# Streaming encoder step on one core: modulation by row blocks of w_ada on four column groups, with the low-rank projection in the same stage

## The reference

```python
mod = jax.nn.silu(c.astype(jnp.float32)) @ P['w_ada'][l] + P['b_ada'][l]
shift, scale, gate = jnp.split(mod[:, None, :], 3, axis=-1)
h = rms_norm(x, P['norm_g'][l]) * (1.0 + scale) + shift
proj = h @ P['w_in'][l]
pr, zA, cq, ckv, kr, zB, sq, sk, sv, zC, gates = _split(proj, IN_SIZES)
yA, S1, shift1 = rwkv7_branch(pr, shift0, S0, P, l)
...
xs = p_shift + (prev - p_shift) * P['rwkv_mu'][l]
r, k, v, wd, ad = _split(xs, RWKV_SIZES)
w_log = -jax.nn.softplus(-(P['rwkv_w0'][l] + jnp.tanh(wd) @ P['rwkv_w_up'][l])) - 0.5
```

## Time and profile before

| | |
|---|---|
| median of 3 runs | 4972.09 us (4970.42 to 4978.52) |
| the profiled execution | 4968.3 us, its span 4966.6 us |
| PE (TensorE, matmuls) busy | 4478.2 us, 90% |
| DVE (VectorE) busy | 2228.7 us, 45% |
| ACT (ScalarE) busy | 1621.3 us, 33% |
| POOL (GpSimd) busy | 722.7 us, 15% |
| mean granted TensorE clock | 0.959 of full speed |
| DMA, mean over the span | 59 GB/s |

### The profile page before, as it was taken

The page is one execution under the profiler, slowest core; times in us unless marked ns, Lnnn a source line. Parts: engine busy times, 40 slices in busy tenths (PEclk is TensorE's granted clock), DMA queues, the critical chain, the costliest instruction groups (busy, mean ns, idle before and its releaser), DMA issues. The chain is left out here.

```text
span 4966.6 us, 75992 instructions
## 1 busy us (share of the span) xinstructions
PE 4478.2 (90%) x29584; PEld 3069.2 (62%) x29584; DVE 2228.7 (45%) x4666; ACT 1621.3 (33%) x3854; POOL 722.7 (15%) x938
## 2 busy tenths in 40 slices
PE   6898888888989989999968898988899899899999
PEld 2556656556756667777425566565567666677774
DVE  2364555245544463434223556552455344634342
ACT  2332333345543341212023333333355333412110
POOL 0010010000001005543000100100000010055430
PEclk9998999999999999999989999999899999999999
DMA  5100110210012203232240101102100121132222
GB/s 213 26 13 22 33 14 23 81 48 25 16 49 74 63 23 127 87 104 73 82 171 26 14 25 29 16 21 81 51 22 15 49 85 56 33 118 98 99 78 68
DMA packets 151028, 291.40 MB, mean 59 GB/s; under 512 B 53332, under 2 KB 79188, under 8 KB 145830
## 3 DMA queue, kind: packets, MB, share of 16 engines
q1 hardware_dynamic: 150552, 281.75, 17.9%
q10 hardware_dynamic: 112, 4.72, 0.3%
HBM read 239.08 MB, written 52.06 MB: 59 GB/s over the span
## 5 line engine op out<-in xcount | busy, mean ns | idle before, releaser
L1014 PE MATMUL banks<-hT,w_piece 128*128 128x384 f32 x1536 | 560.7, 508 | 3.3 <-ACT raw L1118 3.1
L1014 PEld LDWEIGHTS banks<-hT,w_piece 128*128 128x128 f32 x1536 | 287.0, 198 | 178.5 <-issue 24.5
L2197 PE MATMUL banks<-hT,w_piece 128*128 128x384 f32 x1056 | 354.1, 489 | 1.4 <-ACT sb_gate_raw L2307 1.4
L2197 PEld LDWEIGHTS banks<-hT,w_piece 128*128 128x128 f32 x1056 | 196.1, 190 | 141.4 <-issue 16.6
L2548 PE MATMUL banks<-hT,mergedT 128*128 128x512 f32 x576 | 247.5, 592 | 0.0
L1963 DVE SCALAR_TENSOR_TENSOR keysT<-banks,gains,rstd 64x128 f32<-64x128 f32 (+1 forms) x272 | 112.1, 412 | 249.8 <-ACT rstd L1877 247.3
L2594 DVE TENSOR_TENSOR gate_quarters<-gate_kept,banks 128x288 f32<-128x288 f32 x144 | 65.4, 454 | 314.7 <-PE banks L2489 309.7
L2557 ACT ACTIVATE gate_kept<-banks 128x288 f32<-128x288 f32 x144 | 59.2, 411 | 437.0 <-PE banks L2489 437.0
L2548 PEld LDWEIGHTS banks<-hT,mergedT 128*128 128x128 f32 x576 | 109.4, 190 | 137.0 <-issue 136.8
L2369 DVE TENSOR_TENSOR_SCAN left<-pass,zero 128x384 f32<-128x384 f32 (+7 forms) x144 | 189.8, 1318 | 5.0
L2594 DVE TENSOR_TENSOR branch_quarters<-branch_kept,banks 128x288 f32<-128x288 f32 x144 | 65.5, 455 | 267.7 <-PE banks L2489 267.7
(11 more groups left out here) (386 smaller groups left out, 9552.3 us busy)
## 6 DMA issues: line engine op xcount, KB each, us to landing
w_piece<-in_w_cols SPq DMA_DIRECT2D x66, 512.0 KB, 4.6
w_ada<-in_w_ada SPq DMA_DIRECT2D x12, 2048.0 KB, 9.8
w_gate_ahead<-in_w_cols SPq DMA_DIRECT2D x48, 512.0 KB, 4.3
w_branch<-in_w_br SPq DMA_DIRECT2D x96, 256.0 KB, 2.8
w_gate<-in_w_cols SPq DMA_DIRECT2D x48, 512.0 KB, 4.3
y_branch<-y_gated SPq DMA_DIRECT2D x12, 1152.0 KB
sb_cached_keysT<-in_sbkT SPq DMA_DIRECT2D x8, 1024.0 KB, 7.1
sb_cached_values<-in_sbv SPq DMA_DIRECT2D x8, 1024.0 KB, 5.2
```

The source lines that it names most:

```text
L1014: last = mm(dst, w[0 if kind in ("k", "v") else 1][:, k, :], hT[:, k, c], start=(k == 0), stop=(k == KD - 1))
L2197: last = mm(ps[:, bank[n], 0:TG], w_of[wn][:, k, :], hT[:, k, TG * g:TG * g + TG], start=(k == 0), stop=(k == KD - 1))
```

## The change

- `c` is loaded, put through SiLU and turned in the stage of the constants, once for both layers, into `conditioningT`, whose 32 columns hold the nine and zeros. The load of `c` stands ahead of that of the constants.
- `w_ada` stays in rows. SyncE loads blocks of 128 rows by 2048 columns (shift and scale; 1 MB, four buffers), four ahead of x and four behind it. For each block TensorE does four matmuls, one for each 512 columns; the q-th writes PSUM partitions 32q to 32q + 31 of the same bank, so that the four use different groups of 32 columns of the array. Eight blocks accumulate. One addition of a 128 by 512 bias replaces four, and four transposes of 128 by 128 replace 16 small ones.
- The tiles of x are transposed behind the blocks k = 3 to 7, by the table `MOD_TILES`.
- The gate's 1024 columns come in four transfers of two row blocks each, as the buffers get free; group q holds the sum over rows 256q to 256q + 255. The bias is added to the four partial sums (it is zero except in group 0), and the matrices `selp` and `sels` add the groups while they spread the rows.
- The projection of the first `rwkv` stage moves into this stage, in three pieces between that work (`lora`); its tile order follows the scaling of `hT`. ScalarE evicts it and the gate rows. The stage of its own goes.
- The loads of `load_first` move into this stage, behind the gate's weights. The raw last columns are copied to `lora_ends` and stored from the next stage. The zeroing of `scores_r_sample` moves to GpSimd there.

```diff
-        with S.stage("consts_loaded",) as (block, sb, (consts_loaded,)):
+        cT = sbt("conditioningT", [P, KD, 32])
...
+                sp.dma_start(c[:, :], A["c_all"]).then_inc(c_loaded, 16)
                 sp.dma_start(cst[:, :], A["consts"][:, 0:CONST_RESIDENT]).then_inc(consts_loaded, 16)
...
+MOD_TILES = {3: (0, 1, 2), 4: (3, 4), 5: (5, 6), 6: (7,), 7: (8,)}
...
+            def load_w(k):
+                if k >= 4:
+                    sp.wait_ge(mod_used, k - 3)
+                sp.dma_start(w[k % 4][:, :], A["w_ada"][l, k, :, 0:2 * D]).then_inc(w_loaded[k % 4], 16)
...
+            for k in range(4):
+                load_w(k)
             sp.wait_ge(x_copied, 32)
...
+            for k in range(4, KD):
+                load_w(k)
+            sp.dma_start(w_lora[:, :, :], A["w_cols"][l, G_LORA]).then_inc(lora_loaded, 16)
...
+            for q in range(4):
+                sp.wait_ge(mod_used, 5 + q)
+                sp.dma_start(w[q][:, :].rearrange("p (k n) -> p k n", k=2), A["w_ada"][l, 2 * q:2 * q + 2, :, 2 * D:3 * D].rearrange("k p n -> p k n")).then_inc(w_loaded[q], 16)
+            sp.dma_start(bgate[:, :], A["b_gate"][l]).then_inc(bg_loaded, 16)
+            count = load_first(sp, A, l, con, E, None, 0, first_loaded)
             sp.wait_ge(rows_copied, 4)
             sp.dma_start(gates, gate[:, :, :]).then_inc(gates_stored, 16)
+            sp.wait_ge(first_loaded, count)
             sp.wait_ge(gates_stored, 16)
...
+            def lora(n):
+                c = slice(TG * n, TG * n + TG)
...
+                for x in range(KD):
+                    k = x // 2 + KD // 2 * (x % 2)
+                    if n == 0:
+                        pe.wait_ge(act_scaled if x % 2 else dve_scaled, x // 2 + 1)
+                    last = mm(ps[:, 2 + n, 0:TG], w_lora[:, k, :], hT[:, k, c], start=(x == 0), stop=(x == KD - 1))
+                last.then_inc(projected, 1)
+
+            for k in range(KD):
+                pe.wait_ge(w_loaded[k % 4], 16 * (k // 4 + 1))
+                for q in range(4):
+                    last = mm(ps[32 * q:32 * q + 32, 0, :], cT[:, k, :], w[k % 4][:, 512 * q:512 * q + 512], start=(k == 0), stop=(k == KD - 1))
+                last.then_inc(mod_used, 1)
+                for i in MOD_TILES.get(k, ()):
...
+            pe.wait_ge(mod_added, 1)
+            for x in range(4):
+                last = nc.tensor.transpose(ps[:, 1, P * x:P * x + P], mod[:, P * x:P * x + P], ident)
+            last.then_inc(modT_ready, 1)
+            lora(0)
+            pe.wait_ge(modT_copied, 1)
+            for j in range(2):
+                for kk in range(2):
+                    for q in range(4):
+                        if j == 0 and kk == 0:
+                            pe.wait_ge(w_loaded[q], 48)
+                        last = mm(ps[32 * q:32 * q + 32, j, :], cT[:, 2 * q + kk, :], w[q][:, D * kk + 512 * j:D * kk + 512 * j + 512], start=(kk == 0), stop=(kk == 1))
+                last.then_inc(gate_ready, 1)
+            lora(1)
+            for j in range(4):
+                sel = con("selp") if j < 2 else con("sels")
...
+                mm(ps[:, (5, 6, 7, 2)[j], :], sel, part[:, 512 * (j % 2):512 * (j % 2) + 512], start=True, stop=True).then_inc(rows_ready, 1)
+            lora(2)
```

304 lines of the change are left out of this document (141 added, 163 removed).

## The result

The changed kernel took **4919.51 us** (median of 5 runs, 4906.57 to 4924.44) against 4970.42 us (5 runs, 4953.44 to 4978.52) for the kernel before in the same session: ratio 0.9895, 95% interval 0.987 to 0.9921. Faster, then, by some 51 us (39 to 65 by the interval), where 80 were forecast. 4919.5 lies inside the range, near its upper end, and the question is why it lies there.

A forecast was written before the change was run, and what follows sets the result against it. Bound taken: the chain of hand-overs between TensorE, ScalarE and DMA in the modulation and projection stages. Savings of 38.5 us in layer 1 and 41.9 in layer 0 sum to 80.4, giving 4891 us, range 4875 to 4921.

The forecast's parts named there:

- Conditioning out of the layer: Layer 1's start: without c's work and two small loads ahead, first x tiles land at 17.8 us, 1.4 us taken off.
- ScalarE's chain: Modulation: first scaled copy after 5.4 us instead of 6.7, tile 8 ready 24.3 us after x lands, DMA covered.
- Column groups: Modulation's w_ada matmuls: four groups run 2.7 at a time, 1.3 us per row block, 5.1 us for the gate.
- End of the modulation: Layer 1, last tile through projection and token shift to the boundary: ends 61.7 us after x lands, before 96.3.
- Moved transfers: Loads behind the gate weights and gate-row store cost nothing; the last columns' store, 7.3 us of boundary, hides in the next stage.
- Layer 0: Program start: constants wait behind the copy of x until 17.2 us; matmul behind both stages at 99.2 instead of 141.1.
- Rival A: Layer 0's start: constants not held up by the copy, x lands at about 33 us; 4.5 us less, 4887; chance 0.22.
- Rival B: Modulation: column groups don't overlap, gate 13.7 us instead of 5.1; 13 us a layer more, 4917; chance 0.12.
- Rival C: Gate, rows and two projections: TensorE stays at the lower granted clock; 17.5 us a layer more, 4926; chance 0.06.
- Rival D: Modulation: switching column groups drains the array, slower than before; 80 us a layer more, 5051 us; chance 0.01.
- the second sentence of the first part: Outside the modulation and projection stages, the rest of the 4966.6 us span is the same code.

The follow-up runs named there:

- e6: Changed kernel with all w_ada matmuls but the first of each sum sent to the first column group: 4940.8 us, ratio 0.992.
- e9: Changed kernel with the stores of the last columns asked for and awaited again at the end of the modulation's stage: 4935.1 us, ratio 0.9931.
- e5: Changed kernel with c loaded on ScalarE's queue ahead of the copy of x, constants first on SyncE's: 4896.4 us, ratio 0.9859.
- e1: The changed kernel run once more, unaltered: 4918.1 us, ratio 0.9874 against the kernel before.
- e3: Changed kernel with SyncE's first transfer of each layer held back by three small GpSimd memsets: 4910.1 us, ratio 0.9875.
- e2: Kernel before with its tiles at the on-chip addresses that the change gives them: 4974.6 us, ratio 0.9996.
- e4: Kernel before with SyncE's first transfer of each layer held back by three small GpSimd memsets: 4968.0 us, ratio 0.9982.
- e12: Changed kernel with c on ScalarE's queue, never-read matmuls in idle time, and stores of k's last columns asked for one wait sooner: 4864.1 us, ratio 0.9799.

## Why the prediction was right, and where it was not

1. **Conditioning out of the layer: right.** X0 17.5 us after the first issue in layer 1 (17.8 forecast).
2. **ScalarE's chain: right.** 5.4 us to the first scaled copy, the last one over 24.8 us after X0 (24.3). No block waited for DMA behind it.
3. **Column groups: right in kind, mis-sized.** 2.7 at a time was taken between bounds of 1 and 4; the gate took 3.64 us instead of 5.1 and a block 1.06 instead of 1.3, so 13.7 / (3.64 - 0.17) = 3.9 at a time. The upper bound was nearly the truth, and e6 shows the other end. The estimate from the Trainium skill (TensorE: Matmul & The Clock Gate, the speedup of three column groups) gave 5.7 us for the gate; the measurement decides for 3.64.
4. **End of the modulation: right, though two errors cancel, which is luck.** The scalings began at 29.7 us after X0 (29.1), and the first projection ran 7.09 us at the lower clock and ended 1.6 late against the sum with its ramp; the gate gave 1.5 back. The third projection ended at 55.3 us (55.3), the tanh at 60.5 (60.5), L1033 began at 61.3 (61.7). From the tanh's end to L1033 it took 0.8 us, forecast 1.2, before 4.9; e9 shows that the boundary is short because no store is awaited there.
5. **Moved transfers: right.** The four issues of the gate weights lie on SyncE's queue from 2491.98 to 2506.64 us, as buffers come free, and TensorE did not wait for them; the loads behind them were there before SyncE asked. What the term missed is the next stage's own store, see below.
6. **Layer 0: right within 1.4 us** (100.6 for 99.2). The choice of the side, that the constants would now be held up and `c` not, was the one that mattered: 19.8 us for 17.2 forecast. Rival A did not come in the changed kernel (18.5 us from issue to landing). But the prediction gave a wrong reason against it. It read the rule of the Trainium skill (DMA: Bandwidth & Descriptors, Queues, rings and completion order), turns between queues packet by packet, as one that lets a small load in soon, and `c`'s 11 us as a refutation. The packets of both traces show such turns: 16 packets of the one, 16 of the other, over and over in the changed kernel, and in the kernel before `c`'s nine packets begin between 9.9 and 13.1 us, among packets of the copy that take 2.8 to 3.5 us each. What the prediction did not have is how long a packet of the copy holds an engine. e5 then created rival A's situation by another order of issue: 3.5 us less, where it had 4.5.

Rival B (groups in series) had 4917, close to what was measured, and is refuted all the same: a number that fits is not a mechanism. Rival C saw the clock as the danger but in the wrong place: the gate, the rows and two projections ran at the upper level. Rival D did not come: transposes on the full array begin 0.07 us before the modelled end of a block on four groups (2503.97 against 2504.04). The starts of single matmuls leave room for 0.1 us at a change: the first transpose begins 0.52 us after the block's last matmul, where the next four of a gate or block begin 0.43 us after the ones ahead; but from one tile of transposes to the next, with no change of form, it also takes 0.22 instead of 0.11. The Trainium skill (TensorEngine Tiling, Key Properties) has a drain at a change of the tiling mode; if these 0.1 us are one, it is smaller than the 0.17 that the prediction put on it.

**The step that failed** is the second sentence of the first part, "the rest of the 4966.6 us span is the same code", together with the sum's silent conclusion that the same code takes the same time. The head gained 79.7 us; the whole gained 52 to 63 by the ratios of three comparisons (0.9895, 0.9874 and, with 3 us held back, 0.9875). That the range held the result is luck: it reached so far only towards rivals B and C, for reasons that did not occur.

What took its place, by the profiles of e1 to e9 and the first two: six after-type ones (after, e1, e3, e5, e6, e9) against three before-type ones (before, e2, e4). The rest took 4727.7 us for 4716.3 in the mean, 11.4 more, and that has two parts that repeat. **The stage behind the modulation** took 86.6 for 79.9 us in layer 0 and 84.9 for 82.5 in layer 1; most of it is the wait for the store of k's last columns, which took 2 to 4 us longer to land; e12 took that wait away, and the stages fell to 78.7 and 78.6. I had counted the moved transfers, but not asked how much slack the next stage's own store had. Why it lands later was not found. Single packets of it are slower (see above), the tiles' places on the chip don't do it (e2 waits 7.5 us, before 7.3), and e9, with the moved stores back in their place, waits as long as after (12.1 us); places in DRAM were not tested. **Latent attention** took 384 to 385 us in 11 of 12 layers for 377 in 5 of 6, the stage ahead of it 159.6 for 163.4 (but in e9's layer 1, which had 162.9 and 376.8): together some 4 us a layer where both have their usual durations, 2.4 in the means, all of it in TensorE's busy time at the lower clock. The fused stages show both of their durations in both types, with sums of 706 to 737 us (e1 alone is 19 us above the first profile of the same kernel): noise between executions that one profile each can't tell from an effect. By these means the change is worth 79.7 - 11.4 = 68 us; the medians say 51 and 59, with intervals that reach to 65 and 80, so some 10 us may lie in the draw of few runs. Why latent attention has its longer duration so much oftener after the change stays open. A start held back by 2 to 4 us did not move it; the added matmuls, far ahead of it, moved it in both kernels, and in opposite directions.

## What to carry to other kernels

A gain worked out for one stage is paid in full only if the stages behind it run at the same granted clock. In this kernel the same code had two durations (a fused stage 113 to 118 or 119 to 123 us, latent attention 377 or 384 to 385); what chooses between them was not found. So cut the profile into the changed part and the rest, compare the rest by busy time and granted clock first, and if it moved, try a few idle-time matmuls in both kernels before explaining the difference by the change. Ask which of the first transfers stands ahead of a large copy: half a microsecond of issue order decided whether the constants were there by 7.2 or at 19.8 us (e5), though only 3.5 us of it reached the end of the head, since the weights then waited for the copy instead. And where a stage's transfers move, look for waits in the next stage that were nearly covered.

## What the runs showed that was not expected

- Fifty matmuls whose result is never read made this kernel 23 us faster by the ratios (34 by the medians; 18 in the kernel before), with 150 to 190 us less at the lower clock. The Trainium skill (TensorE: Matmul & The Clock Gate, Part 1) has the ramp penalty at under 1% of a typical kernel's span and varying by run. That is about one ramp; here the clock fell 52 times in the changed kernel, and stood at its lower level for 446 of 4909 us. The difference between the two kernels in unchanged code, 22.3 us, is 0.5% of the span, but more than a quarter of this change's gain.
- Four column groups of 32 run 3.9 matmuls at a time in float32 (16 matmuls of 512 columns in 3.64 us), with at most 0.1 us at a change to the full array's transposes and back.
- A load of 36 KB asked for together with a DRAM-to-DRAM copy landed within 2.6 us; the constants (0.9 MB), 0.46 us behind that copy and on another queue, needed 18.5 us, packet by packet in turn with the copy's.
- A store of nine columns awaited at a stage's end costs 7.4 to 8.8 us, and one of the same kind in the middle of a stage took 11.8 us from issue to use in the kernel before and 15.9 in the changed one, with the same code around it.
